# First memory attention of a two-block layer: the second memory's turn placed ahead of the values, the values in other banks, the query norms as a chain of their own

## The reference, cut to what matters

```python
def memory_cross_attention(h, m, w_q, w_kv, q_g, k_g, w_o):
    q = rmsnorm(heads(h @ w_q, 4), q_g)          # 4 heads of 128
    k, v = jnp.split(m @ w_kv, 2, axis=-1)
    k = rmsnorm(heads(k, 4), k_g)
    v = heads(v, 4)
    s = jnp.einsum("bqhd,bkhd->bhqk", q, k) * 128 ** -0.5
    p = jax.nn.softmax(s, axis=-1)
    return jnp.einsum("bhqk,bkhd->bqhd", p, v).reshape(B, S, 512) @ w_o

x = x + memory_cross_attention(rmsnorm(x, norm_xq), rmsnorm(mem, norm_mem), ...)
mem_n = rmsnorm_2(mem_2, mem_g_2)      # second memory, used by the second block
k2    = mem_n @ xa_wkv[:, 0:1024]      # its keys; two of four pieces are computed here
```

## The kernel before, in words

| chunk | what | PSUM banks before | read out by |
|---|---|---|---|
| 43, 44 | first memory's keys | (2,3), (0,1) | `add`, VectorE |
| 45, 46 | queries mq | (2,3), (0,1) | `add`, VectorE (line 2219) |
| 47, 48 | values mv, two halves of one sum (line 1347) | (6,7) | `copy`, ScalarE (line 1730), behind 48 |
| 49, 50 | second memory's keys xk (lines 1328, 1331) | (2,3), (0,1) | `add`, VectorE |
| 51, 52 | output product w_mo (line 1362) | (0,1,2,3) | `resid`, VectorE |

## Time and profile before

### The profile page before, as it was taken

The page is one execution under the profiler, slowest core; times in us unless marked ns, Lnnn a source line. Parts: engine busy times, 40 slices in busy tenths (PEclk is TensorE's granted clock), DMA queues, the critical chain, the costliest instruction groups (busy, mean ns, idle before and its releaser), DMA issues.

```text
span 1171.4 us, 16802 instructions
## 1 busy us (share of the span) xinstructions
PE 1145.2 (98%) x6765; PEld 999.7 (85%) x6765; DVE 812.5 (69%) x881; ACT 622.3 (53%) x801; POOL 82.1 (7%) x114
## 2 busy tenths in 40 slices
PE   8999999999999999999999999999999998999997
PEld 7978898889987799999888888888777887888886
DVE  6897658756878568787548777547776747777743
ACT  7666446436478466565345444436456547444432
POOL 7101100200000000000000000002700000000000
PEclk9999999999999999999999999999999999999999
DMA  8654333334665354655655655555633534665560
GB/s 259 190 158 147 99 106 110 109 108 156 220 198 181 108 163 156 204 169 191 216 179 181 210 179 186 200 195 177 201 116 127 180 108 127 194 202 182 179 214 36
DMA packets 144420, 193.95 MB, mean 166 GB/s; under 512 B 6168, under 2 KB 121240, under 8 KB 144344
## 3 DMA queue, kind: packets, MB, share of 16 engines
q1 hardware_dynamic: 143144, 188.43, 49.7%
q0 software_dynamic: 1200, 4.46, 1.1%
HBM read 191.82 MB, written 1.05 MB: 165 GB/s over the span
## 4 chain that ended last, share of the span: by engine, by line
PE 83%; DVE 10%; ACT 4%; issue 2%; DMA 0%; DVEq 0%; ACTq 0%
PE banks L1328 23%; PE banks L1362 19%; PE banks L1310 13%; PE banks L1331 11%; DVE wlo L1920 4%; PE banks L1347 3%; PE banks L1338 2%; PE banks L1589 1%; PE banks L1477 1%; ACT whi L1649 1%; PE banks L1464 1%; PE banks L1376 1%; PE banks L1547 1%; DMA x_tok<-in_x 0%; DVE x_tok L2193 0%
## 5 line engine op out<-in xcount | busy, mean ns | idle before, releaser
L1920 DVE TENSOR_TENSOR wlo<-raw,whi 128x2048 fp32r<-128x2048 f32 (+1 forms) x178 | 406.5, 2291 | 122.5 <-ACT whi L1649 122.4
L1649 ACT ACTIVATE whi<-raw 128x2048 fp32r<-128x2048 f32 (+1 forms) x179 | 340.1, 1903 | 248.3 <-PE banks L1331 146.0
L1328 PE MATMUL banks<-xhl,whi 128*128 128x512 f32 x1232 | 396.2, 403 | 2.7 <-DVE y5l L2248 1.8
L1331 PEld LDWEIGHTS banks<-xhl,wlo 128*128 128x128 f32 x1232 | 231.4, 188 | 54.6
L1331 PE MATMUL banks<-xhl,wlo 128*128 128x256 f32 x1232 | 242.6, 278 | 0.0
L1328 PEld LDWEIGHTS banks<-xhl,whi 128*128 128x128 f32 x1232 | 188.9, 189 | 10.3 <-issue 5.6
L1310 PE MATMUL banks<-xhl,whi 128*128 128x256 f32 x912 | 165.5, 284 | 1.3 <-DVE xhl L1947 0.7
L1310 PEld LDWEIGHTS banks<-xhl,whi 128*128 128x128 f32 x912 | 142.0, 192 | 2.1 <-DVE xhl L1947 1.1
L1310 PE MATMUL banks<-xhl,wlo 128*128 128x256 f32 x456 | 129.0, 283 | 0.0
L1362 PE MATMUL banks<-whi,hh 128*128 128x512 f32 x264 | 102.9, 390 | 0.0
L1362 PE MATMUL banks<-wlo,hh 128*128 128x512 f32 x264 | 102.7, 389 | 0.0
(11 more groups left out here) (368 smaller groups left out, 1531.9 us busy)
## 6 DMA issues: line engine op xcount, KB each, us to landing
raw<-in_w_in SPq DMA_DIRECT2D x40, 1024.0 KB, 5.3
raw<-in_w_up SPq DMA_DIRECT2D x22, 1024.0 KB, 5.8
raw<-in_ffn_w_gate SPq DMA_DIRECT2D x22, 1024.0 KB, 5.3
raw<-in_ffn_w_up SPq DMA_DIRECT2D x22, 1024.0 KB, 5.3
raw<-in_ffn_w_down SPq DMA_DIRECT2D x22, 1024.0 KB, 5.0
raw<-in_w_down SPq DMA_DIRECT2D x11, 1024.0 KB, 5.6
raw<-in_w_out SPq DMA_DIRECT2D x8, 1024.0 KB, 5.2
raw<-in_xa_wkv SPq DMA_DIRECT2D x8, 1024.0 KB, 5.7
```

What stands on the lines that cost most here:

```text
L1328: pe.matmul(bank(b[m]), wh[:, k, m * P:(m + 1) * P], both[:, k, :, :].rearrange("p a t -> p (a t)"), start=(k == 0), stop=(k == KD - 1), s ...
L1331: ins = pe.matmul(bank(b[m])[:, 0:T], wl[:, k, m * P:(m + 1) * P], Xh[:, k, :], start=False, stop=(k == KD - 1), skip_group_check=True)
L1649: act.activation(columns(whi, c, part), columns(raw, c, part), ACT.Copy).then_inc(act_done, 1)
L1920: dve.tensor_tensor(columns(wlo, c, part), columns(raw, c, part), columns(whi, c, part), ALU.subtract).then_inc(dve_done, 1)
```

## The change

The values go to banks 2 and 3. The turn of the second memory goes to banks 4 to 7 and is written between chunks 46 and 47, no longer as a side chain. The two query norms become a chain of their own (they no longer wait for the products of the key norms) and enter the side list ahead of chunk 46. The first group of the turn waits for the root of every norm job whose sum stands before it; a query sum that stands behind the turn waits for the turn's last low part. The scores wait for the key products too, and those of heads 0 and 1 for the turn's last low part, but no longer for the copy of the values.

```diff
-    vals("w_mkv", 512, "m1", "vcopy", (6, 7), to="mv")
+    vals("w_mkv", 512, "m1", "vcopy", (2, 3), to="mv")
...
     def input_of(step):
-        if name == "sc" and args == ["mem", 1]:
-            return pl.ended.get(("copy", max(c for c, ch in enumerate(chunks) if ch.get("to") == "mv")), 1e9)
...
     norm_scale("mem_g_2")
+    side.append(hn("mq0", "mq1"))
     mm(c + 1)
     c += 2
-    drain()
     stage[0] = "mem"
-    side.append(hn("mq0", "mq1"))
-    turn_m2 = [[lambda: norm_turn("mem_g_2", 0, "m2")]]
-    side.append(turn_m2)
-    finished[id(turn_m2)] = max(pl.ended["nd", "mem_g_2", 1], pl.ended["add", c - 1])
-    for lane in range(2):
-        side.append(heads_of("mem", [lane, lane + 2]))
+    norm_turn("mem_g_2", 4, "m2")
+    lanes = [heads_of("mem", [lane, lane + 2]) for lane in range(2)]
+    for lane in lanes:
+        side.append(lane)
     mm(c)
     mm(c + 1)
     c += 2
-    while turn_m2:
-        place(turn_m2.pop(0)[0])
...
-        for jobs in ((...), (...), ("mk0", "mk1", "mq0", "mq1")):
+        for jobs in ((...), (...), ("mk0", "mk1"), ("mq0", "mq1")):
             HN_BEFORE |= dict(zip(jobs[1:], jobs))
...
             def nt(name, j):
+                if name == "mem_g_2" and j == 0:
+                    for job in ("mk0", "mk1", "mq0", "mq1"):
+                        if at("hn_sum", job) < at("nt", name, 0):
+                            pe.wait_ge(act_done, at("hn_r", job))
...
             def hn_sum(job):
+                if job[:2] == "mq":
+                    behind = at("hn_sum", job) > at("nt", "mem_g_2", 0)
+                    pe.wait_ge(dve_done, at("nl", "mem_g_2" if behind else "norm_xq", KD - 1))
...
             def sc(kind, h):
                 elif kind == "mem":
                     pe.wait_ge(dve_done, at("hn_mul", f"mq{h // 2}"))
-                    if h == 1:
-                        pe.wait_ge(act_done, at("copy", chunk_of("mv", None)))
+                    pe.wait_ge(dve_done, at("hn_mul", f"mk{h // 2}"))
+                    if h < 2:
+                        pe.wait_ge(dve_done, at("nl", "mem_g_2", KD - 1))
```

More of the change, by code:

```diff
@@ L1068, in two_blocks_kernel @@
         HN_BEFORE = {}
-        for jobs in (("gq0", "gk0", "gq1", "gk1", "go0", "go1"), ("fq0", "fq1", "fk0", "fk1"), ("mk0", "mk1", "mq0", "mq1")):
+        for jobs in (("gq0", "gk0", "gq1", "gk1", "go0", "go1"), ("fq0", "fq1", "fk0", "fk1"), ("mk0", "mk1"), ("mq0", "mq1")):
             HN_BEFORE |= dict(zip(jobs[1:], jobs))
```

## The result

| | before | after |
|---|---|---|
| median (lowest, highest), us | 1174.59 (1174.39, 1175.78), 8 runs | 1178.53 (1177.12, 1178.65), 8 runs |
| ratio after to before | | 1.0033, 95% interval 1.0023 to 1.0042 |
| the profiled execution, span | 1171.4 | 1175.4 |
| mean granted clock | 0.998 | 0.996 |

The change is 3.94 us slower by the medians, 4.0 by the two spans. Both profiled executions are quick ones of their kernel: 1173.07, not one of the eight above, lies 1.5 under the old median; 1177.12, the lowest of its eight, lies 1.4 under the new one. The forecast was 1177.5, plus 2.9.

What follows compares the result with a forecast made beforehand. TensorE, working through nearly the whole span, and its chain of waits were taken as the bound. Waits of 3.3 + 0.3 + 0.1 + 0.7 + 2.6 = 7.0 us replace 3.9, less 0.2: plus 2.9, 1177.5 us, range 1174.6 to 1180.2.

Steps and rivals of the forecast that it cites:

- the clock: Rival: TensorE's 3.1 us idle before the turn halves the clock for chunk 47, up to 5.5 us, 1183.0; chance 0.04.
- The orders: Derived instruction order of TensorE, ScalarE and VectorE from chunk 45 on, with no instruction added or removed and no load late.
- Step 1: Turn ahead of the values: its first group waits 3.3 us for ScalarE's root of mk1, starting at 365.75.
- Step 2: Query norm behind the turn: sum of mq0 waits 0.3 us for the turn's last low part, starting at 373.2 or 373.3.
- Step 3: Values in banks 2 and 3: chunk 49 waits for their copy, 0.1 us exposed behind scores 0 and 1, 1.5 uncovered.
- Step 4: The heads: value product 1 waits 0.7 us, and chunk 51 waits 2.6, starting at 400.7 against 398.38.
- Step 5: From chunk 51 to chunk 52, which starts at 409.1 against 406.17: plus 2.9 us, passed on to the end.
- The bounds: Turn's wake 0 to 0.5, exposed copy 0 to 1.5, handovers 0.03 to 0.26 each: forecast's case plus 1.8 to 4.8 us.
- the heads catching up: Rival: root of mq1 before high part 51, step 4's waits of 0.7 and 2.6 vanish: minus 0.4, 1174.2; chance 0.20.
- a longer chain: Rival: the chain to chunk 51 stretches, for instance low 52 waiting for high 52: 2 us more, 1179.6; chance 0.10.
- the planner placed the turn and the norms as derived: Rival denied here: the planner places turn or norms otherwise and the turn ends up where it was, 1174.6; chance 0.04.

Runs made afterwards that it cites:

- bank4_last: Changed kernel with the turn's four groups in banks 5, 6, 7, 4, so only the last waits for the root of mk1; 1178.42 us.
- sq_late: Changed kernel with the query chain put into the side list behind the turn instead of ahead of chunk 46; 1181.32 us.
- fill_turn: Changed kernel with 26 dummy transposes on TensorE ahead of the turn's wait for the root of the second key norm; 1178.00 us.
- fill_both: Changed kernel with dummy transposes on TensorE at both idle stretches, 26 ahead of the turn and 20 ahead of chunk 51; 1176.12 us.
- root_q_first: Changed kernel with high part 51 put behind the root of mq1 on ScalarE; 1177.87 us.
- fill_out: Changed kernel with 20 dummy transposes on TensorE ahead of chunk 51's wait for the low outputs; 1178.22 us.
- chain_only: Old kernel with only the query norms made a chain of their own, entering the side list ahead of chunk 46; 1175.27 us.
- old_margin10: Old kernel with the planner's margin for a link in this stage at 1.0 us in place of 0.5; 1173.84 us.

## Why the prediction was right, and where its sum was short

The direction and the mechanism of the waits held, 1178.53 lies in the range, and the forecast of plus 2.9 compares with 3.94. That the range held the total is in part luck: its upper side was meant for handovers and an exposed copy, which stayed small, and what filled it was the clock, whose case the prediction left outside.

- *The orders* were as derived, each engine's.
- *Step 1*: 3.3 between starts; 3.14 idle in the profile, ended by the root.
- *Step 2*: sum of mq0 at 373.2 or 373.3 with 0.3 of wait; 373.16, with 0.2 between starts and none in the list. That the two waits are one price is shown by bank4_last.
- *Step 3*: scores (379.31) covered the copy (379.56), and no wait for it is in the list; sq_late shows what it costs uncovered, 1.3.
- *Step 4*: value product 1 waiting 0.7, chunk 51 at 400.7; the weight loads show 0.5 there, and chunk 51 was at 400.65. VectorE's terms there, from 387.3 on, add up to 397.7, not 397.6; maxima 3 ended at 397.45.
- *Step 5*: plus 2.9; without a fall of the clock plus 2.72 (fill_turn) and 2.52 (fill_both). What the sum lacked is the clock. It stood among the rivals at 0.04, for the stretch before the turn alone and at up to 5.5 us. The term was mis-sized twice: a fall costs 1.6 before chunk 52 and 2.3 at the turn, and it is no rare case but goes with the idle time. TensorE had 3.1 and 2.5 us of idle time 32 us apart in place of 0.9 and 2.2. In the profiled pair 2.7 of waits and 1.6 of clock make the 4.3 between the marks. The medians differ by 1.2 more than the waits, in line with it, but both hold falls from elsewhere too. The row that I read as a sign against it (full clock behind 1.18 us busy in 3.40) was one execution, and the same trace holds a sign for it that I overlooked. Behind a wait of 1.6 us, with little work ahead of it, the clock fell with matmuls running:

```profile
976.00:978.00 2.00, 0.65 (x5) 0.65 (x6) 1.92 (x6) 1.60 (x5) 0.41 (x1) 0.96 0.00 0
978.00:980.00 2.00, 2.00 (x11) 2.00 (x11) 1.16 (x5) 1.87 (x8) 0.23 (x2) 0.50 0.54 186
```

- *The bounds*: with the copy exposed by up to 1.5, the upper terms add up to plus 6.1 and not 4.8, and the range's plus 5.6 leaves out the last of that. The copy was covered, so nothing came near it.

The Trainium skill, "TensorE: Matmul & The Clock Gate", section "What's actually happening", says that the default state is throttled and activity releases it. fill_both agrees: transposes of no use kept the clock up in the attention of its profiled execution and gave 2.4 us back.

- *The rivals*: the heads catching up was refuted by root_q_first in the form it was given, with this root ahead of high 51; a longer chain did not occur, and the planner placed the turn and the norms as derived. So the place of the root of mk1 makes the wait at the turn, while moving the root of mq1 alone brings chunk 51 only 0.3 earlier.

## What to carry to other kernels

Before a step is moved ahead in TensorE's queue, look at which entry of ScalarE's queue releases it and what stands in front of that entry: with 2.5 us of high part and square in front of one root this move cost 2.7 us at the mark, with that root first 0.7, and with the other root early too and a wider margin it won 2.1. When a wait disappears by a new bank or a dropped semaphore, ask for the next wait on the same chain, since two waits behind one root are paid once. And a wait on TensorE can cost more than its length: the clock may fall behind it, and that shows in some executions only.

## What the runs showed of the hardware

The granted clock fell at idle stretches of the same length in some executions and not in others: after 3.1 us idle before the turn it stayed full in the changed kernel and fell in fill_out; after about 2.5 us idle before chunk 51 it fell in the changed kernel and stayed full in fill_turn. A kernel's executions differ by it: 27 of the old one, measured together, ran from 1172.82 at a clock of 0.997 to 1175.94 at 0.995. A comparison of single executions can be off by up to 3 us, and differences in the clock go along with it. The start-to-start marks don't have this noise where the window's clock is 1.00: they told 0.65 (chain_only) and 0.67 us (old_margin10) from nothing, where the intervals of the medians didn't. Shorter idle time can be enough: TensorE waited 1.6 us in one piece before 977.35 in the old kernel, and the clock fell there or shortly behind in all twelve profiled executions. Why it falls in one execution and not in the next was not settled.
